# A three-pass fp32 model kernel on one core: the two attentions of a stage change places, and the first loads come in pieces

## The reference, cut to what matters

```python
def swiglu(h, w_gu, w_down):
    g, u = jnp.split(h @ w_gu, 2, axis=-1)
    return (jax.nn.silu(g) * u) @ w_down
...
# second block (SEQ 256, 4 + 4 heads of 128)
        h = rms_norm_2(x, g_mix_norm[l]) * (1.0 + sc_m) + sh_m
        proj = h @ w_in[l]
        (q_a, k_a, v_a, q_i, k_i, w_i, q_b, k_b, v_b, gate_a, gate_b) = jnp.split(proj, split_at, axis=-1)
...
        o_a = dsa_attention(q_a, k_a, v_a, q_i, k_i, w_i)   # keys selected: top 64 by an index score
        o_b = moba_attention(q_b, k_b, v_b)                 # here one block of 256: plain causal attention
        merged = (jax.nn.sigmoid(gate_a) * (o_a @ w_br_dsa[l])
                  + jax.nn.sigmoid(gate_b) * (o_b @ w_br_moba[l]))
        x = x + gt_m * (merged @ w_out[l])
```

## Time and profile before

| what | us |
|---|---|
| median of 3 runs (lowest, highest) | 1517.40 (1513.64, 1519.47) |
| the profiled execution | 1511.95 |
| its span, first to last instruction | 1510.1 |
| TensorE busy (matmul) | 1457.1 |
| VectorE busy | 1053.0 |
| ScalarE busy | 697.8 |
| GpSimd busy | 29.0 |

### The profile page before, as it was taken

How to read it: one execution, slowest core, us unless ns; L and a number is a source line. 1 busy time by engine, 2 the same in 40 slices (tenths; PEclk the granted TensorE clock), 3 DMA queues, 4 the chain that set the end, 5 groups by cost and what they waited for, 6 DMA issues and landing times. The chain is left out here.

```text
span 1510.1 us, 28569 instructions
## 1 busy us (share of the span) xinstructions
PE 1457.1 (96%) x11627; PEld 1415.9 (94%) x11627; DVE 1053.0 (70%) x1436; ACT 697.8 (46%) x897; POOL 29.0 (2%) x58
## 2 busy tenths in 40 slices
PE   5999999999999999999999989999999899999999
PEld 5999999999999999999988879999988789999999
DVE  5666878777667786667877667667878755776653
ACT  5444344355444354443544655443435665554441
POOL 0000100000000000001000000000000000000000
PEclk9999999999999999999999999999999999999999
DMA  7544754525556745448343116557633344454550
GB/s 298 191 167 169 264 208 154 183 110 223 178 186 230 270 155 181 167 178 298 122 165 127 70 57 251 185 204 251 237 114 138 114 165 168 168 196 167 187 203 29
DMA packets 41674, 269.08 MB, mean 178 GB/s; under 512 B 4673, under 2 KB 5825, under 8 KB 12273
## 3 DMA queue, kind: packets, MB, share of 16 engines
q1 hardware_dynamic: 33120, 240.31, 43.7%
q0 software_dynamic: 7312, 26.44, 5.0%
q10 hardware_dynamic: 1152, 1.05, 0.2%
HBM read 266.73 MB, written 1.05 MB: 177 GB/s over the span
## 5 line engine op out<-in xcount | busy, mean ns | idle before, releaser
L385 PE MATMUL ps<-x_hi,w_hi 128*128 128x272 f32 (+2 forms) x2296 | 664.9, 290 | 29.0 <-DVE w_lo L1031 16.6
L386 PE MATMUL ps<-x_lo,w_hi 128*128 128x272 f32 (+2 forms) x2296 | 654.5, 285 | 0.0
L387 PE MATMUL ps<-x_hi,w_lo 128*128 128x272 f32 (+2 forms) x2296 | 654.3, 285 | 0.0
L1817 ACT ACTIVATE w_hi<-raw_weights 128x2048 fp32r<-128x2048 f32 x222 | 423.7, 1913 | 314.9 <-PE ps L387 314.2
L1031 DVE TENSOR_TENSOR w_lo<-raw_weights,w_hi 128x2048 fp32r<-128x2048 f32 x196 | 447.1, 2290 | 165.8 <-ACT w_hi L1817 165.3
L385 PEld LDWEIGHTS ps<-x_hi,w_hi 128*128 128x128 f32 x2296 | 436.1, 190 | 33.2 <-DVE w_lo L1031 16.6
L386 PEld LDWEIGHTS ps<-x_lo,w_hi 128*128 128x128 f32 x2296 | 436.3, 190 | 0.5
L387 PEld LDWEIGHTS ps<-x_hi,w_lo 128*128 128x128 f32 x2296 | 436.1, 190 | 0.0
L385 PE MATMUL ps<-a_hi,w_hi 128*128 128x272 f32 x592 | 169.6, 286 | 0.0
L386 PE MATMUL ps<-a_lo,w_hi 128*128 128x272 f32 x592 | 169.6, 286 | 0.0
L387 PE MATMUL ps<-a_hi,w_lo 128*128 128x272 f32 x592 | 169.6, 286 | 0.0
(11 more groups left out here) (247 smaller groups left out, 1533.4 us busy)
## 6 DMA issues: line engine op xcount, KB each, us to landing
raw_weights<-w_units SPq DMA_DIRECT2D x228, 1024.0 KB, 4.8
mod_w<-mod_units POOLq DMA_DIRECT2D x48, 512.0 KB, 5.0
h<-x_in SPq DMA_DIRECT2D x1, 1088.0 KB, 5.7
out<-h ACTq DMA_DIRECT2D x8, 128.0 KB, 1.9
tab<-tables POOLq DMA_DIRECT2D x1, 512.0 KB, 9.4
tab<-constants POOLq DMA_DIRECT2D x1, 272.0 KB, 3.0
con<-constants POOLq DMA_DIRECT2D x2, 128.0 KB, 6.2
f<-constants POOLq DMA_DIRECT2D x1, 136.0 KB, 7.1
```

Source lines behind the costliest of these rows:

```text
L385: pe.matmul(dst, wh, hi, start=start, stop=False)
L386: pe.matmul(dst, wh, lo, start=False, stop=False)
L387: return pe.matmul(dst, wl, hi, start=False, stop=stop)
L1817: act.activation(w_hi[:, u % RING, :], raw[:, u % RING, :], ACT.Copy).then_inc(S["hi_ready"], 1)
```

## The change

Two things are done together.

In the w_in stage the two attentions change places: SP loads the units of the row passes in the order v, q, k of b and then of a (the twelve units are the same), so that the steps 0 to 3 are attention b, with the mask as bias, and the steps 4 to 7 are attention a, with `sel`. Of `take_best(1, ...)` five rounds move behind the first attention's begin and `select` moves behind the last rotation. In the second unit of a row pass the order is all of query half 0, then all of query half 1. Keys are handled by query half: squares, root, reciprocal and scale of half 0, then of half 1. The turns are placed earlier. `store_p2(3)` and `store_o2(3)` come ahead of `row_squares(2, ...)`. Group 7's first unit runs as `first_gates`: blocks 0 and 1 for four k-tiles, then blocks 2 and 3. From `br_dsa` on, all bank numbers are turned by four (`shift`).

At the start h comes in three parts and unit 0 in four pieces, the latter on ScalarE's queue; the high and low parts of k-tile k and of quarter k of unit 0 are made in turn, TensorE waits for each quarter alone, the squares come later, ScalarE's first table load no longer waits for h, and 20 matmuls of zeros run on TensorE before anything has landed.

```diff
+WARM = 20
+H_PARTS = ((0, 2), (2, 4), (4, 8))
...
     def bank(self, t):
         first = 2 * GROUP if self.name == "w_in" else GROUP
-        return (t - self.t0) % 4 if self.quad and t >= self.t0 + first else t % 8
+        return (t - self.t0) % 4 if self.quad and t >= self.t0 + first else (t + self.shift) % 8
...
+        plan["shift"] = GROUP
         stage("proj", "br_dsa", 2, 8, SEQ, True)
...
+        ROW_GAIN, ROW_ROOTS = (2, 3, 0, 1), (0, 1, 3, 4)
...
-            sp.dma_start(h[:, :, :], x_in).then_inc(h_loaded, 16)
-            for s in range(RING):
+            for (first, end), loaded in zip(H_PARTS, h_loaded):
+                sp.dma_start(h[:, first:end, :], x_in[:, first:end, :]).then_inc(loaded, 16)
+            for s in range(1, RING):
                 sp.dma_start(raw[:, s, :], w_units[s]).then_inc(raw_loaded[s], 16)
...
+                    for u in range(RING * turned[0], RING * (turned[-1] + 1)):
+                        n = u - first_row
+                        from_u = first_row + (n + ROW_GROUPS) % (2 * ROW_GROUPS) if 0 <= n < 2 * ROW_GROUPS else u
+                        sp.wait_ge(S["lo_ready"], u - RING + 1)
+                        sp.dma_start(raw[:, u % RING, :], w_units[from_u]).then_inc(raw_loaded[u % RING], 16)
...
+                        if in_pieces:
+                            pe.wait_ge(*((S["lo_piece"], k + 1) if k < 3 else (S["lo_ready"], 1)))
...
+            pe.wait_ge(S["warm_ready"], 1)
+            for n in range(WARM):
+                ins = pe.matmul(ps[:, 0, 0:TOK], ident_b[:, :], mask[:, :], start=True, stop=True)
+            ins.then_inc(S["warmed"], 1)
             gate_up(0, 0)
...
+                    order = [(kk, qt) for kk in range(4) for qt in range(2)]
+                    if half == 1:
+                        order = [(kk, qt) for qt in range(2) for kk in range(4)]
...
+            def first_gates(between):
+
+                u = w_in.u0 + 15
+                pe.wait_ge(S["lo_ready"], u + 1)
+                for n in range(8):
+                    k, pair = n % 4, n // 4
+                    for m in (2 * pair, 2 * pair + 1):
+                        t = w_in.tile(7) + m
+                        if k == 0:
+                            wait_bank(w_in, t)
+                        ins = three_pass(ps[:, w_in.bank(t), 0:SEQ], u % RING, (k * GROUP + m) * P,
+                                         x_hi[:, k, 0:SEQ], x_lo[:, k, 0:SEQ], k == 0, False)
+                    if n % 2 == 1:
+                        for job in between.get(n // 2, ()):
                             job()
...
-            rows(2, {4: [lambda: turn_rows(0, 0)], 6: [lambda: turn_rows(0, 1)]})
-            rows(3, {6: [lambda: turn_rows(1, 0)], 7: [lambda: turn_rows(1, 1)]})
+            rows(2, {2: [lambda: turn_rows(0, 0)], 4: [lambda: turn_rows(0, 1)]})
+            rows(3, {2: [lambda: turn_rows(1, 0)], 5: [lambda: turn_rows(1, 1)]})
             rows(4, {
-                1: [lambda: scores2(0)],
-                3: [lambda: scores2(1), lambda: turn_p2(0)], 4: [lambda: values2(0)],
-                5: [lambda: scores2(2), lambda: turn_p2(1)], 6: [lambda: values2(1)],
-                7: [lambda: scores2(3), lambda: turn_p2(2)]})
+                0: [lambda: scores2(0)],
+                2: [lambda: scores2(1), lambda: turn_p2(0)], 3: [lambda: values2(0)],
+                4: [lambda: scores2(2), lambda: turn_p2(1)], 5: [lambda: values2(1)],
+                6: [lambda: scores2(3), lambda: turn_p2(2)], 7: [lambda: values2(2)]})
             rows(5, {
-                0: [lambda: values2(2)], 1: [lambda: turn_p2(3)], 2: [lambda: values2(3)],
+                0: [lambda: turn_p2(3)], 2: [lambda: values2(3)],
                 4: [lambda: turn_rows(2, 0)], 6: [lambda: turn_rows(2, 1)]})
-            group(w_in, 7, xs, between={5: [lambda: turn_rows(3, 0)], 7: [lambda: turn_rows(3, 1)]})
+            first_gates({2: [lambda: turn_rows(3, 0)]})
+            group(w_in, 7, xs, between={5: [lambda: turn_rows(3, 1)]}, halves=(1,))
...
+            for k in range(4):
+                first_low(k)
+                first_piece(k)
+            nxt[0] = 1
+            add_square(1, TOK)
             split_to(2)
+            for k in range(4, 8):
+                first_low(k)
+                add_square(k - 2, TOK)
...
+            normalise(3)
+            row_rope(2, 0)
+            low_half()
+            row_rope(2, 1)
+            low_half()
+            row_roots(2)
             low_half()
             take_best(1, 2)
...
+            low_half()
+
+            row_roots(3, 0)
+            row_rope(3, 0)
+            row_roots(3, 1)
+            low_half()
+            row_rope(3, 1)
+            low_half()
+            take_best(1, TOPK // 8 - 5)
             for qt in range(2):
                 select(qt)
...
+            for n in range(4):
+                cols = slice(n * UNIT // 4, (n + 1) * UNIT // 4)
+                act.dma_start(raw[:, 0, cols], w_units[0, :, cols]).then_inc(first_loaded[n], 16)
+            act.wait_ge(S["eps_ready"], 1)
+            act.activation(eps[:, 2:3], eps[:, 0:1], ACT.Square)
...
+            for k in range(4):
+                first_high(k)
+                first_piece(k)
+            nxt[0] = 1
+            for m in range(2):
+                square(m, h[:, m, :], TOK)
+            split_to(2)
+            for k in range(4, 8):
+                first_high(k)
+                square(k - 2, h[:, k - 2, :], TOK)
...
+            store_p2(3)
+            store_o2(3)
 
             row_squares(2, 0)
             row_squares(2, 1)
             row_std(2)
-            store_p2(3)
-            store_o2(3)
             split()
```

More of the change, by code:

```diff
@@ L86, in __init__ @@
         self.after_tail = plan["after_tail"]
-        self.first_fresh = plan["quad"] or quad_banks
+        self.shift = plan["shift"]
+        self.first_fresh = (plan["quad"] or quad_banks) and not self.shift
         plan["after_tail"] = tail
@@ L417, in rows_free, with group @@
                     pe.wait_ge(S["row_scaled"], n - 1 + qt + 1)
-            def group(st, g, xs, i=0, x_base=None, bank_busy=None, between=None):
-                for half in range(2):
+            def group(st, g, xs, i=0, x_base=None, bank_busy=None, between=None, halves=(0, 1)):
+                for half in halves:
                     u = st.u0 + 2 * g + half + (1 if st.name == "w_in" else 0)
-                    pe.wait_ge(S["lo_ready"], u + 1 + 4 * i)
+                    in_pieces = st.u0 == 0 and g == 0 and half == 0
+                    if not in_pieces:
+                        pe.wait_ge(S["lo_ready"], u + 1 + 4 * i)
                     for kk in range(4):
@@ new lines, in rows @@
+                        if k == 0 and j == 0:
+                            pe.wait_ge(S["tile_evicted"], w_in.evicted(w_in.t0 + GROUP))
+                        elif k == 0 and j == 1 and qt == 0:
+                            pe.wait_ge(S["mod_evicted"], MOD_PARTS)
+                        elif k == 0 and j == 1:
+                            pe.wait_ge(S["rotation_read"], ki_rotated[0])
+                        elif k == 0:
+                            rows_free(j - 2, qt)
+                        dst = ps[:, ROW_BANKS[j % 2][qt], :]
@@ new lines, in rows @@
+                        xh, xl = (x[:, k, qt * P:(qt + 1) * P] for x in (x_hi, x_lo))
+                        pe.matmul(dst, xh, wh, start=k == 0, stop=False)
+                        pe.matmul(dst, xl, wh, start=False, stop=False)
+                        ins = pe.matmul(dst, xh, wl, start=False, stop=k == KT - 1)
+                        if k == KT - 1:
+                            ins.then_inc(S["rows_done"], 1)
+                        if n % 2 == 1:
+                            for job in between.get(4 * half + n // 2, ()):
+                                job()
@@ L953, in scores2 @@
                               start=True, stop=False)
-                    ins = pe.matmul(ps[:, 4 + comp, 0 if which == 0 else n - P:n], ident_b[:, :], bias,
+                    ins = pe.matmul(ps[:, 4 + comp, 0 if which == 1 else n - P:n], ident_b[:, :], bias,
                                     start=False, stop=True)
@@ L1288, in _, with first_low, first_piece @@
             dve.tensor_tensor(lam[:, 0:2], vec[:, V_LAM:V_LAM + 4:2], vec[:, V_LAM + 1:V_LAM + 4:2], ALU.mult)
-            dve.wait_ge(h_loaded, 16)
-            update_and_prepare(TOK, 0, None, ln(0, 0), None, False, stages["up", 0], update=False,
-                               between={5: lambda: split_to(1)})
-            split_to(2)
+            def first_low(k):
+                for (first, _), loaded in zip(H_PARTS, h_loaded):
+                    if k == first:
+                        dve.wait_ge(loaded, 16)
+                dve.wait_ge(S["x_hi_ready"], c.up("x_hi_ready"))
+                dve.scalar_tensor_tensor(x_lo[:, k, :TOK], h[:, k, :], ln(0, 0)[:, k:k + 1],
```

(23 more changed lines are left out.)

149 lines of the change are left out of this document (78 added, 71 removed).

## The result

| kernel | us, median (lowest to highest) | ratio to before, 95% interval |
|---|---|---|
| before, beside it | 1517.22 (1513.64 to 1521.93, 6 runs) | |
| changed | 1503.60 (1501.70 to 1507.11, 6 runs) | 0.9915 [0.9893, 0.9938] |
| changed, second comparison | 1507.37 (6 runs; before 1514.44, 29 runs) | 0.9955 [0.9937, 0.9972] |
| changed, third comparison | 1507.39 (6 runs; before 1516.91, 14 runs) | 0.9937 [0.9920, 0.9955] |

The change makes the kernel faster by 13.6, 7.1 and 9.5 us in three comparisons. The forecast was 12.5 us, 1505 us for the median, with a range from 1498 to 1512 that holds all three. By the bound of 0.5% the first (0.85%) and the third (0.63%, with an interval that reaches down to 0.45%) are faster, and the second, 0.45%, is within it.

A forecast was written before the change was run, and what follows sets the result against it. TensorE was taken as the bound, busy 1457.1 of 1510.1 us, leaving 53 us of stands and half-rate stretches to win. Terms 6.1 + 2.8 + 3.6 = 12.5 us from 1517.4 gave 1505 us, range 1498 to 1512.

The forecast's parts named there:

- The start, 6.1 us: Kernel start: with unit 0 and h in pieces, k-tiles 4 and 5 end at 21.4 instead of 27.5 us.
- I take the full rate, because the engines are saturated: Loads at the start: small pieces cost nothing; at half rate 2.6 us more for unit 0, 5.2 with h.
- Rival C: Start: the pieces are slow, unit 1 lands 3 to 5 us late, start worth 1 to 3.5 us; chance 0.17.
- The row passes, 2.8 us: w_in: waits removed by the new orders, less new stands for the last keys; gain 2.8 us, bounds 0 to 9.
- the waits of 1.2 and 1.8 us go: Row passes in w_in: TensorE's waits for turned rows (1.2 us) and ahead of the first scores (1.8 us) vanish.
- The end of the stage, 3.6 us: Branch projection after w_in: begins in free banks, 2.1 us, without the half-rate stretch, 1.5 us; bounds 2 and 4.
- The sum, 12.5 us: Whole kernel: 6.1 + 2.8 + 3.6 us gained, 1505 us for the median, 1499.5 for a profiled execution.
- forecast A: Whole kernel: each part within 3 us of its term, 9.5 to 16 us gained, 1501.5 to 1508; chance 0.60.
- B: First gates in w_in: TensorE does not stand, ScalarE and VectorE steps estimated 2 to 5 us too slow; 1499; chance 0.13.
- D: Row passes give nothing: later squares cost what the removed waits gave, slow stretch longer; 1509.5; chance 0.05.
- E: Last pass: each us its half 1 keys are ready after 1215.4 costs TensorE one; slower, 1520 or more; chance 0.05.

The follow-up runs named there:

- experiment 5: The changed kernel with unit 0 loaded by one transfer instead of four pieces, h still in three parts: 1505.10 us, ratio 0.9924.
- experiment 4: The changed kernel without the turn of the banks by four after w_in: 1507.70 us, ratio 0.9959.
- (7): The changed kernel with two selection rounds moved into VectorE's idle time and the squares of queries a ahead of a store: 1501.76 us, ratio 0.9908.
- (11): The changed kernel with the old orders back in each row pass's second half and in the first gates: 1505.66 us, ratio 0.9938.
- experiment 8: The kernel of (7) with the last keys' squares and roots of both token tiles ahead of both scalings: 1501.15 us, ratio 0.9908.

## Why the prediction held, term by term

**The start, 6.1 us.** Measured 6.3 us at the third reciprocal (239.88 against a mean of 233.6 of the eight traces with pieces and 20 warm-up matmuls) and 5.9 us at the one at 915 (mean 909.3). The size is right, the way to it was not, and that the two agree is luck: 1.3 us too much up to the first reciprocal and 1.5 us left out behind it. "I take the full rate, because the engines are saturated" failed: 250 GB/s arrived from 2 to 6 us instead of 341, pieces landed late (11.4 us for the last), and unit 1 came at 12.9, 14.2 and 13.7 us in the three traces and not at 11.8. The first matmul was at 8.95 us and not near 7, since the first part of h took until 7.1 us. I had k-tiles 0 to 3 done at 15 us if TensorE ran at half rate all the while, and then a stand of 2 to 3.5 us. The 15 is a slip: by the rate of the earlier trace rows (18 matmuls in 4.2 us) 48 matmuls take 11.2 us, to 18.2. In the first trace they took until 17.1 us, the stand was 0.36 us, and no slow stretch followed it. The second and third are done at 16.0 and 16.2 us, have stands of 2.7 and 2.0 us, each with a stretch at half rate behind it, and first reciprocals 1.5 and 1.1 us later. From the first to the third reciprocal before takes 206.6 us and the eight 204.6 to 206.0, mean 205.1, where before has a stretch at half rate from 34 to 38 us that I had not counted; that makes the 4.8 us at the first reciprocal 6.3 at the third. The change does not always remove it: five of the nine traces with pieces have such a stretch from 30 us on and take 205.4 to 206.0 us, the four without one take 204.6. Rival C had the right mechanism with too high a price: 1.1 to 2.4 us on unit 1 and 2.1 on the start, not 3 to 5. Its sign, unit 1 at 14 us or later, is met in one of the nine traces. The rule of the Trainium skill ("DMA: Bandwidth & Descriptors", section Bandwidth: batch loads to at least 1 MiB) points the way that experiment 5 went, where 1 MB in four pieces was slower to land than in one; its size here is the 2.1 us of the runs. The constants went out at 11.7 us and not at 8, since GpSimd waits for the whole of unit 0. The lambda product waited 0.9 us for VectorE's mask copy, which I had 1 us ahead; in the second and third trace it did not wait.

**The row passes, 2.8 us.** Measured 1.8 us: from the start of w_in to the last gate's matmul it is 171.1 and 172.5 us in the two traces with the old attention, 169.3 to 170.7 in eight with the new (means 171.8 and 170.0). The removed waits went as told, and pass 5 ends 4.2 us earlier (4.6 forecast). The stands for row_k were forecast as 1.9 + 3.0 and measured as 1.84 + 2.82 us, with the cause as told: squares behind the moved store and VectorE late at the roots. What the step "the waits of 1.2 and 1.8 us go" left out is a new wait of 1.0 us for turned rows in pass 5 (L932): the rotation of queries a stands behind the same late squares. About 0.4 us of the missing 1 us is lost by the end of pass 5. The rest lies behind it and is not shown: the two old traces alone are 1.4 us apart there.

**The end of the stage, 3.6 us.** Measured 2.1 + 1.3 = 3.4 us (experiment 4), by the steps as told; the half rate, forecast at 1.5 us, comes in two of the three traces with the stand.

**The sum, 12.5 us.** The start gives 5.9 to 6.3 us. For w_in, five pairs of an old and a new trace have equal steps in both branch projections; they differ by 4.1 to 5.3 us, mean 4.6, where 2.8 + 3.6 = 6.4 were forecast. That makes 10.5 to 10.9 us, and what is missing to 12.5 lies in w_in. The three comparisons of medians gave 13.6, 7.1 and 9.5, a mean of 10.1; the 7.1 lies below the 9.5 to 16 us of forecast A. Their scatter fits the step of two sizes: it moves the stage at 915 us by 6.5 us and the first one by 4 to 6, and the 29 runs of before alone reach from 1510.2 to 1523.2. The profiled executions fit it too: the five with a slow stage at 915 us lie 2.8 to 6.0 us above the median of their kernel, the seven with the small step in both columns between 5.3 us below and 0.9 above. That it explains all of the scatter is not shown. Whether the changed kernel falls into the slow step more often is open. Its stage at 915 us is slow in two of three traces and in five of the twelve with the new start, against none of two with the old, too few to tell.

**The rivals.** B fell: keys were late, and it took moving them (7) to gain 4.2 us. D fell for the change as a whole, since the row passes gave 1.8 us; but its mechanism, later squares that cost what the removed waits gave, is what the exchange without the new orders shows (11). E's mechanism is the one that was found at work, at the size forecast and no more.

## What to carry to other kernels

Before a stage is judged, compare the spacing of its matmuls between executions: here one value or the other moved a stage by 6.5 us, more than any term of the sum. When a stand for one engine is shortened, look what the waiting engine needs next from the same one: experiment 8 took 1.7 us out of one stand and found them all in the next. Splitting the first unit k-tile by k-tile gained 2.5 us here, loading it in pieces cost 2.1; of the rest of the start, 4.5 us, the shares are open.

## What the runs showed that was not expected

- The start-to-start distance of matmuls takes one of two values per stage and execution, with the granted clock at 1.00: 113.3 or 117.8 ns at 256 columns, 123.3 or 126.7 ns at 272 columns. It holds through the stage and can change at the next one. The same kernel had both. What sets it is open.
- 1 MB in one transfer landed at 6.0 us; in four transfers of 256 KB its last part came at 11.4 us, beside the same other loads. From 2 to 6 us all loads together moved 341 GB/s with the one transfer and 250 GB/s with the four.
- Twenty matmuls from 1.2 to 5.9 us, then 3 us without any: the next ones went at half rate until 13.9 us, and until 11.6 to 14.9 us in the other traces in which they begin at 8.5 to 9 us; behind a single warm-up matmul it was 13.0 us.
- A stand of 2.3 us was followed by half rate in two traces and by full rate in one. At the start, behind k-tile 3, stands of 1.8 to 2.7 us had a stretch at half rate behind them in four traces, and stands of 0.4 to 1.7 us in five had none.
